# Differential attention, last pair of heads: the copy of turned weights ahead of the next exponentials, low parts of heads between maxima and sums

## The reference

```python
def diff_attn_core(q, k, v, lam):
    s = jnp.einsum('bqhcd,bkhcd->bhcqk', q, k) * DIFF_HEAD_DIM ** -0.5
    p = jax.nn.softmax(s, axis=-1)
    w = p[:, :, 0] - lam * p[:, :, 1]
    return jnp.einsum('bhqk,bkhe->bqhe', w, v)
...
    o = rms_norm(o, subln_gain) * (1.0 - lam_init)
    return o.reshape(b, l, D_MODEL) @ w_out
```

## Time and profile before

| | before |
|---|---|
| median of three runs | 2472.69 us |
| the profiled execution | 2477.41 us |
| its span | 2475.3 us |
| TensorE busy | 2404.4 us (97%) |
| VectorE busy | 1298.8 us (52%) |
| ScalarE busy | 879.4 us (36%) |
| GpSimd busy | 374.9 us (15%) |

### The profile page before, as it was taken

One profiled execution on the slowest core, in us unless ns is written; L12 is line 12 of the kernel. 1 busy time (PEld: TensorE's weight loads), 2 busy tenths in 40 slices (PEclk: granted clock), 3 DMA queues, 4 the chain that ended last, 5 costly groups with the idle time before them and its releaser, 6 DMA issues.

```text
span 2475.3 us, 34710 instructions
## 1 busy us (share of the span) xinstructions
PE 2404.4 (97%) x14354; PEld 2009.5 (81%) x14354; DVE 1298.8 (52%) x2101; ACT 879.4 (36%) x1499; POOL 374.9 (15%) x301
## 2 busy tenths in 40 slices
PE   8999999999999999999999999999999999999999
PEld 6778888888887777656888887988989878877788
DVE  3775625543535776875333336366565445554433
ACT  4331211111224444444222224364545333444422
POOL 0210000000014444501000001143343410000000
PEclk9999999999999999999999999999999999999999
DMA  9834334434321111012333332221222121121222
GB/s 324 204 94 125 119 103 130 126 119 118 104 68 35 52 38 48 35 44 76 92 96 102 95 93 86 69 69 52 69 69 78 60 69 52 52 69 52 77 94 111
DMA packets 252744, 220.79 MB, mean 89 GB/s; under 512 B 7480, under 2 KB 243443, under 8 KB 252204
## 3 DMA queue, kind: packets, MB, share of 16 engines
q1 hardware_dynamic: 249072, 217.92, 28.7%
q10 hardware_dynamic: 3260, 0.58, 0.1%
q0 software_dynamic: 256, 0.07, 0.0%
HBM read 214.26 MB, written 6.29 MB: 89 GB/s over the span
## 4 chain that ended last, share of the span: by engine, by line
PE 59%; ACT 3%; DVE 3%; issue 2%; POOL 1%; DVEq 0%; ACTq 0%; POOLq 0%
PE two L685 10%; PE bank L1354 5%; PE bank L1545 4%; PE bank L685 4%; PE bank L1350 3%; PE bank L1331 3%; PE two L1285 3%; PE bank L1526 2%; PE bank L1051 2%; PE two L1156 2%; PE bank L1182 2%; PE two L1565 2%; PE bank L1021 1%; PE bank L1033 1%; PE two L1297 1%
## 5 line engine op out<-in xcount | busy, mean ns | idle before, releaser
L2568 DVE TENSOR_TENSOR wL<-ring,wH 128x512 fp32r<-128x512 f32 x224 | 182.5, 829 | 225.3 <-ACT wH L1840 225.1
L1831 ACT ACTIVATE wH<-ring 128x2048 fp32r<-128x2048 f32 (+1 forms) x80 | 149.1, 1864 | 272.4 <-PE bank L690 73.4
L2557 DVE TENSOR_TENSOR wL<-ring,wH 128x2048 fp32r<-128x2048 f32 (+1 forms) x80 | 180.4, 2255 | 82.2 <-ACT wH L1831 82.0
L685 PE MATMUL two<-h1H,wH 128*128 128x512 f32 x496 | 195.5, 394 | 0.0
L685 PE MATMUL two<-h1H,wL 128*128 128x512 f32 x496 | 193.4, 390 | 0.0
L685 PE MATMUL two<-h1L,wH 128*128 128x512 f32 x496 | 193.3, 390 | 0.0
L1840 ACT ACTIVATE wH<-ring 128x512 fp32r<-128x512 f32 x224 | 133.6, 623 | 58.8 <-PE bank L1331 21.1
L1909 ACT ACTIVATE gateS<-two 128x512 f32<-128x512 f32 x44 | 26.3, 598 | 332.2 <-PE bank L690 142.0
L2661 DVE SCALAR_TENSOR_TENSOR xT<-two,ada,xT 128x512 f32<-128x512 f32 (+1 forms) x48 | 30.6, 679 | 186.2 <-PE bank L690 66.3
L3204 POOL TENSOR_TENSOR rstd<-rstd,sq 128x768 f32<-128x768 f32 (+1 forms) x15 | 30.4, 2024 | 611.4 <-ACT sq L1867 610.2
L1354 PE MATMUL bank<-unH,wH 128*128 128x272 f32 (+1 forms) x368 | 112.2, 305 | 3.9 <-ACT cin L2100 2.1
(11 more groups left out here) (642 smaller groups left out, 6953.5 us busy)
## 6 DMA issues: line engine op xcount, KB each, us to landing
ring<-in_ffn_w_in SPq DMA_DIRECT2D x88, 512.0 KB, 5.1
ring<-in_w_in SPq DMA_DIRECT2D x40, 1024.0 KB, 5.0
ring<-in_w_ada SPq DMA_DIRECT2D x32, 1024.0 KB, 5.2
ring<-in_ffn_w_out SPq DMA_DIRECT2D x16, 1024.0 KB, 5.1
early<-in_w_ada SPq DMA_DIRECT2D x12, 1024.0 KB, 12.0
ring<-in_diff_w_in SPq DMA_DIRECT2D x12, 1024.0 KB, 5.2
ring<-in_w_proj_ssd SPq DMA_DIRECT2D x8, 1024.0 KB, 4.9
ring<-in_ffn_w_out SPq DMA_DIRECT2D x8, 768.0 KB, 4.5
```

Source lines behind the costliest of these rows:

```text
L685: m = nc.tensor.matmul(bank[3 * s + half], w, r[:, 0:LAT], start=i == 0, stop=i == n - 1)
L1831: nc.scalar.activation(hi, raw, ACT.Copy).then_inc(w_hi, 1)
L2557: nc.vector.tensor_tensor(lo, raw, hi.bitcast(F32), ALU.subtract).then_inc(w_lo, 1)
L2568: nc.vector.tensor_tensor(lo, raw, hi.bitcast(F32), ALU.subtract).then_inc(q_lo, 1)
```

## The change

On ScalarE, in the last eight turns (f = 3), `keep_turned(u - 1)` is issued ahead of `weights_of(u)` and not behind it, and so also ahead of `head_raw` and `head_root`. On VectorE, the low parts of heads 2 and 3 are computed in x = 2 between the maxima (and an addition) and `combine`, and not in x = 1 behind `combine`; those of heads 4 and 5 in x = 5 and not in x = 4. Instructions and semaphores stay the same.

```diff
@@ scalar engine
                     for h in range(2):
                         head_hi(h)
+                if f == 3:
+                    keep_turned(u - 1)
                 weights_of(u)
                 if x == 1 and f:
                     head_raw(2 * f - 1)
...
                 if x == 5:
                     head_raw(2 * f)
-                if u:
+                if u and f < 3:
                     keep_turned(u - 1)
@@ vector engine
                 maxima(u)
                 if f == 3:
                     next(out_adds)
+                    if x == 2:
+                        head_lo(2)
+                        head_lo(3)
+                    if x == 5:
+                        head_lo(4)
+                        head_lo(5)
                 combine(u)
...
                 if f == 3:
-                    if x == 1:
-                        head_lo(2)
-                        head_lo(3)
-                    if x == 4:
-                        head_lo(4)
-                        head_lo(5)
                     if x < 2:
```

## The result

The changed kernel takes 2479.42 us (median of 14 executions, 2473.93 to 2484.18) against 2474.01 for the kernel before on the same chips (14, 2471.08 to 2478.78). The ratio is 1.0021, 95% interval 1.0011 to 1.0030: slower by some 5.4 us.

What follows compares the result with a forecast made beforehand. It took a VectorE-ScalarE loop as the bound, with TensorE joining in turns 25 and 29. Schedule +3.9 us plus one clock fall of 1.7 gave +5.6, 2478.3 us against the median 2472.69; range 2473.5 to 2481.5.

Steps and rivals of the forecast that it cites:

- What bounds the turn: Turns 24 to 31: a closed loop between VectorE and ScalarE, 5.93 us without extras; TensorE enters in turns 25 and 29.
- The wait behind the product: Turns 25 and 29: the early WT copy waits behind the head product, so exponentials start at 1052.4 and 1084.7.
- The square: Turns 25 and 29: GpSimd's square of the head product lengthens VectorE's combination by 0.91 us, bounds 0 and 1.04.
- The low parts: VectorE, moved to turns 26 and 29: hide 0.5 us and delay turn 26's sums by 0.7; hidden whole in 29.
- The clock: TensorE's gaps of some 2.4 us, before turn 25's product and part 16: each over one half likely to cost 1.7.
- A: One of TensorE's two gaps lowers its clock: +5.6 us, 2478.3; chance 0.42.
- C: Both of TensorE's gaps lower its clock: +7.3 us, 2480.0; chance 0.28.
- D: Exponentials of turns 25 and 29 lose no time and the gains stand: some −1.6 us, 2471.1; chance 0.07.
- E: The late start is absorbed in the tail, or the change does nothing the end sees: 0 us; chance 0.04.
- B: Neither of TensorE's gaps lowers its clock, only the schedule's loss is left: +3.9 us, 2476.6; chance 0.19.

Runs made afterwards that it cites:

- Mending the gaps: Changed kernel plus products with overwritten results ahead of the waits of turn 25's head product and output part 16: median 2478.09 us against 2480.72 for the changed kernel.

## Why the prediction held, and where not

The prediction was +5.6 us in two parts, 3.9 of schedule and 1.7 of clock; measured are 5.4, and 5.3 and 5.8 in the two other comparisons. That the sum came within 0.2 is in part luck: both of its terms were somewhat too large, and what makes up the difference stays open (below).

- **What bounds the turn**: held. TensorE's waits on the WT copy went and nothing was gained by it, because the loop of maxima, exponentials and combination runs between VectorE and ScalarE: turn 27 to 28 took 6.6 as worked out, 28 to 29 took 5.94.
- **The wait behind the product**: held. Exponentials of turn 25 at 1052.38 (1052.4 forecast) and of turn 29 at 1084.36 (1084.7). Alone these two turns cost 7.0 of 7.1 us, and without them the loss in distance is gone.
- **The square**: the meeting was foreseen, its price was the term that was mis-sized. I took 0.91 for each from the nearest row; it is 0.65. In both cases the GpSimd instruction comes while VectorE multiplies P and then goes ahead of the combination, which ends 0.8 us after it: at 1025.16 against 1024.35 in that row, at 1056.93 against 1056.12 here. The one of that row lasted 1.49 and the square 1.25, which fits the shorter wait. (In that row 1.02 plus what was left of the GpSimd instruction, 1.12, makes 2.14 and not 1.93.) That makes the schedule's part 3.4 and not 3.9, and part 16 comes at 1104.4, not 1105.0. That GpSimd waits too, 1.25 and 1.31 against 1.04, I had not spoken of.
- **The low parts**: held, 0.8 us gained alone. In turn 29, where I called them hidden whole, they cost 0.25: from the maxima of 29 to those of 30 it is 12.23 with them and 11.98 with the copy alone.
- **The clock**: mechanism and size held (7.08 against 5.39, distance 67.3). The chance was too high. I gave each gap a little over one half; the profiles show four of fourteen, an expectation of 1.0 us and not 1.7 (0.98 falls, by the chances of A and C).
- **Rivals**: D, that the exponentials of turns 25 and 29 lose no time, and E are out. Between A (one fall), B (none) and C (two) the single executions vary: of the seven profiles four have none, two have one, one has both. So the likeliest case was B, and A's value came out because it lies near the mean.

What stays open: 3.4 of schedule and 1.0 of clock make 4.4, and the medians differ by 5.3 to 5.8. 4.4 lies within the interval of the ratio (2.7 to 7.4 us). Mending the gaps took 2.6 rather than 1.0. Either the low clock is more frequent than the seven profiles say, or something behind the changed turns takes part.

The granted clocks of all executions bear on the first. Their mean is 0.9956 over 36 of the changed kernel and 0.9948 over 75 of the kernel before (the difference is uncertain by some 0.0005), so as a whole the changed kernel has the higher clock. The two low stretches that only the old order has, half of 3.4 us lost in each, account for 0.0014; the remaining 0.0006 are low clock that the changed kernel has of its own. That is 1.5 us if all of it lies on the path, an estimate with an error of about 1. That is more than the profiles' 1.0 and would make the sum 4.9.

On the second, single profiles differ by more than what is missing. From part 16 to L1264 the three profiles of the changed kernel take 412.2, 412.2 and 415.1, before 412.1; the 415.1 has a low clock behind the tail's gap. From L1264 to the end they take 959.7, 962.3 and 958.9, before 962.2. And the low parts alone, which open neither gap, lie 0.8 us under the kernel before in distance and 1.9 over it in the median (ratio 1.0003). So the last us or so of the difference is within the scatter of the measurements, and its cause isn't shown.

## What to carry to other kernels

Ahead of moving an instruction up in an in-order queue, ask what it waits for in every pass of the loop, not in the usual one: here the early copy was free in six turns and held the exponentials for some 4.6 us in the two turns where a long product stood ahead of its transposes. A wait that ends last before the busiest engine isn't the bound while the loop through the other engines is longer. Work moved next to another engine's work can be slowed by it, as the combination was by the square; moving that work by half a microsecond may only hand the wait to the next instruction.

## What the runs showed of the hardware

While a GpSimd square ran, whichever of VectorE's instructions with two tensor inputs came next was held up and ended some 0.5 to 0.8 us after the square: the combination took 1.67 against 1.02 with the square ahead of it, one split 1.53 against 0.68 with the square ahead of that. A square that came during a combination waited for it and still went ahead of the split behind it: in the kernel with the square moved, turn 29, it took 1.85 and not 1.04, and the combination its usual 1.02.

And gaps of the same length, 2.3 to 2.4 us, at the same place of the same code, were followed by TensorE's low clock in four of fourteen cases, those of 2.6 to 2.7 us in the tail in eight of twelve, but the shorter ones of the old order, 1.75 to 2.13 us ahead of the scores of turns 25 and 27, in all seven. The length of a gap alone doesn't decide.
